# Who makes the low parts of the right operands: VectorE alone, or VectorE and GpSimd in turn

## What is computed

```
first_block:  x += mix(differential attention, forgetting attention) @ w_out
              x += (silu(h2 @ w_gate) * (h2 @ w_up)) @ w_down      # width 2816 = 22 tiles of 128
              rmsnorm
second_block: x += mix(two convolutions, stick-breaking attention) @ w_out
              x += square(relu(h2 @ w_ff1)) @ w_ff2                # width 4096 = 32 tiles of 128
              rmsnorm
```

## Time and profile before

| | us |
|---|---|
| median of 3 runs | 2449.29 (2448.19 to 2449.95) |
| the profiled execution, its own time | 2449.95 |
| its span, first to last instruction | 2447.9 |
| PE busy in the span | 2386.8 (98%) |
| DVE busy | 1906.9 (78%) |
| POOL busy | 1178.2 (48%) |
| mean granted TensorE clock | 0.989 |

### The profile page before, as it was taken

The page is one execution under the profiler, slowest core; times in us unless marked ns, Lnnn a source line. Parts: engine busy times, 40 slices in busy tenths (PEclk is TensorE's granted clock), DMA queues, the critical chain, the costliest instruction groups (busy, mean ns, idle before and its releaser), DMA issues.

```text
span 2447.9 us, 31946 instructions
## 1 busy us (share of the span) xinstructions
PE 2386.8 (98%) x11378; PEld 1953.2 (80%) x11378; DVE 1906.9 (78%) x2456; ACT 1098.3 (45%) x1885; POOL 1178.2 (48%) x798
## 2 busy tenths in 40 slices
PE   9999999999989999999999999999998999999998
PEld 7777788878768888878877878887876888788886
DVE  6777757673699787779979966778289888899976
ACT  6454656562543333344336436555163333544423
POOL 4666542211555555555545463431256555555552
PEclk9999999999999999999999999999998999999998
DMA  4311321232113232355332872223213444654522
GB/s 164 78 54 51 88 61 40 60 116 71 56 48 129 86 112 96 120 177 159 113 94 81 189 171 61 60 60 109 76 57 130 169 144 149 215 181 138 181 78 103
DMA packets 233260, 264.64 MB, mean 108 GB/s; under 512 B 18448, under 2 KB 145168, under 8 KB 232976
## 3 DMA queue, kind: packets, MB, share of 16 engines
q1 hardware_dynamic: 229504, 250.29, 32.5%
q0 software_dynamic: 3168, 11.54, 2.5%
q10 hardware_dynamic: 432, 0.79, 0.1%
HBM read 170.53 MB, written 61.60 MB: 95 GB/s over the span
## 4 chain that ended last, share of the span: by engine, by line
PE 84%; DVE 8%; POOL 3%; ACT 2%; issue 2%; DMA 1%; SPq 0%; POOLq 0%; DVEq 0%; ACTq 0%
PE PS L1768 24%; PE PS L1773 23%; PE PS L1770 23%; PE PS L1866 3%; PE PS L1853 2%; PE PS L1887 2%; PE PS L1884 2%; PE PS L1847 2%; DVE R0f L2173 1%; PE PS L1850 1%; DVE R L2180 1%; POOL stage L2650 0%; DVE R L2249 0%; PE PS L1852 0%; DVE X L2257 0%
## 5 line engine op out<-in xcount | busy, mean ns | idle before, releaser
L1768 PE MATMUL PS<-R,wh 128*128 128x512 f32 x2860 | 1137.4, 398 | 23.3 <-DVE stage L2161 10.8
L2626 POOL TENSOR_TENSOR lows<-values,wh 128x512 fp32r<-128x512 f32 (+2 forms) x483 | 717.5, 1490 | 890.0 <-ACT wh L2378 679.1
L1773 PE MATMUL PS<-R,wh 128*128 128x512 f32 x2860 | 1122.0, 392 | 8.7 <-DVE R L2180 5.9
L1770 PE MATMUL PS<-R,lows 128*128 128x512 f32 x2496 | 977.4, 392 | 1.2 <-POOL lows L2626 1.2
L1768 PEld LDWEIGHTS PS<-R,wh 128*128 128x128 f32 x2860 | 541.2, 189 | 137.8 <-DVE stage L2161 12.7
L1773 PEld LDWEIGHTS PS<-R,wh 128*128 128x128 f32 x2860 | 540.0, 189 | 129.4 <-DVE R L2180 7.1
L2378 ACT ACTIVATE wh<-values 128x512 fp32r<-128x512 f32 (+2 forms) x484 | 299.3, 618 | 580.6 <-PE PS L1773 552.3
L1770 PEld LDWEIGHTS PS<-R,lows 128*128 128x128 f32 x2496 | 471.4, 189 | 93.4 <-issue 3.8
L2257 DVE TENSOR_TENSOR X<-PS,X 128x1024 f32<-128x1024 f32 x168 | 204.2, 1217 | 35.8 <-PE PS L1773 35.3
L2626 POOL TENSOR_TENSOR late_r<-late,wh 128x512 fp32r<-128x512 f32 (+1 forms) x92 | 137.2, 1492 | 113.8 <-DVE values L2155 65.6
L2161 DVE TENSOR_TENSOR stage<-PS,stage 128x512 f32<-128x512 f32 x156 | 105.5, 685 | 64.5 <-PE PS L1773 64.3
(11 more groups left out here) (277 smaller groups left out, 3091.0 us busy)
## 6 DMA issues: line engine op xcount, KB each, us to landing
scr_hid<-R1f SPq DMA_DIRECT2D x177, 256.0 KB, 3.0
R0f<-scr_hid SPq DMA_DIRECT2D x92, 256.0 KB, 3.6
values<-w_in_dram SPq DMA_DIRECT2D x88, 256.0 KB, 2.8
R1f<-scr_hid SPq DMA_DIRECT2D x85, 256.0 KB, 3.3
values<-w_ff_dram SPq DMA_DIRECT2D x62, 256.0 KB, 3.0
values<-w_ff_dram SPq DMA_DIRECT2D x100, 128.0 KB, 2.4
R<-R SPq DMA_DIRECT2D x96, 128.0 KB, 2.3
X<-X POOLq DMA_DIRECT2D x22, 512.0 KB, 5.6
```

The costliest lines, as they stand in the source:

```text
L1768: e.matmul(PS[:, b, :], wh, high, start=s["start"], stop=False, skip_group_check=on)
L1770: e.matmul(PS[:, b, :], wl, high, start=False, stop=False, skip_group_check=on)
L1773: m = e.matmul(PS[:, b, :], wh, low, start=False, stop=s["stop"], skip_group_check=on)
L2626: e.tensor_tensor(T.wl[piece.v][:, 0:m], T.wv[piece.v][:, 0:m], T.wh[:, piece.h, 0:m].bitcast(F), ALU.subtract).then_inc(*sg.up("w_lo", pi ...
```

## The change

Of each pair of operands, the low part of one is now made by POOL and of the other by DVE. Which of the two it is alternates with the product's slot in `FROM_HIDDEN`; for a single operand (the short chunk) even slots go to POOL and odd ones to DVE. In the plain part the second of each pair goes to POOL. The planner then makes new lists for all engines. Nothing else changes: the same operands, loads, high parts and matmuls.

```diff
         def fetch_block(c, name):
             k, rows = todo[c]
             slot = FROM_HIDDEN.index(name)
-            by = ("vector", "vector")
+            by = ("vector", "gpsimd") if slot % 2 else ("gpsimd", "vector")
             fetch((c, slot), [(n, k // 2 + x, slot) for x, n in enumerate(operands(c)[name])], by)
 
         def fetch_plain(x):
             p = (tiles - 4) // 2
-            fetch(("plain", x), [(PLAIN[tag][2 * x + h], p + x // 2, 2 * (x % 2) + h) for h in range(2)], ("vector", "vector"))
+            fetch(("plain", x), [(PLAIN[tag][2 * x + h], p + x // 2, 2 * (x % 2) + h) for h in range(2)], ("vector", "gpsimd"))
```

## The result

The changed kernel takes 2466.51 us (median of 4 runs, 2465.25 to 2467.24), the kernel before 2449.62 beside it: ratio 1.007, 95% interval 1.0058 to 1.0084. It is slower by 0.7%, outside my range, and on the side to which I gave 0.17. The profiled execution took 2464.84 us.

What follows compares the result with a forecast made beforehand. PE was taken as the bound, so only its waits at the seams could give: 2.3 us before the first block products plus 1.25 in the short chunk, 3.55 us less, forecast 2445.7 us against the median; overall range 2439.5 to 2455.

Steps and rivals of the forecast that it cites:

- What POOL takes on: Full chunks: seven more parts, 8.9 to 12.5 us, bring POOL to 28 to 33 of 38.1 us; costed at nothing.
- POOL is late with the weights: Rival, chance 0.13: first weight part late in 22 groups, 0.8 us each, 17 us in all; about 2463 us.
- Both engines get in each other's way: Rival, chance 0.04: full chunks, DVE's parts and sums slowed by POOL; up to 6.3 us a chunk, halfway 2461 us.
- The seam: Before each FFN's first block product: DVE frees the bank sooner, PE waits 1.15 us less, twice 2.3 us.
- The next part takes the gap: Rival, chance 0.17: another ready part precedes the seam's sum, only the short chunk gives 1.25 us; about 2448 us.
- The short chunk: Freeing some 2 us of DVE there removes PE's waits of 0.41 and 0.84 us: 1.25 us less.
- What DVE is rid of: Full chunks: DVE loses seven parts, 6.7 us at the mean, falling from about 37 to 30 us; costed at nothing.
- The clock: At each seam, a shorter wait may keep the clock from falling: 0 to 1.7 us, in the range only.

Runs made afterwards that it cites:

- e3: The changed kernel, planner counting 1779 ns instead of 1379 for POOL's operand part and DVE's as ending after the POOL instruction beside it: 2452.87 us.
- h2: The changed kernel's lists kept, but POOL fills its 89 low parts with zeros in eight pieces of 64 columns instead of the difference: 2445.36 us.
- e2: Lists of the kernel before kept, planned with all parts on DVE; only afterwards the 89 parts are carried into POOL's list: 2448.39 us.
- f2: The changed kernel with the last seven's sum put ahead of the operand parts before it in DVE's list, at both seams: 2466.51 us.
- f4: The kernel before, with the last seven's sum put ahead of the two operand parts before it in each FFN: 2447.82 us.
- e1: The changed kernel with ACT in POOL's place for the 89 parts, writing a plain copy instead of the difference, lists planned anew: 2446.25 us.
- g3: The kernel before, all parts on DVE, planner counting DVE's operand part as ending 0.1 us behind the POOL instruction beside it: 2442.95 us.
- g1: The changed kernel's lists kept, but POOL fills each of its 89 low parts with zeros in one memset instead of the difference: 2444.1 us.
- e4: The changed kernel with the parts of each FFN's first chunk back on DVE, the other 75 on POOL: 2459.13 us.
- g4: The changed kernel with its planner counting 0.4 us more for POOL's operand part and DVE's part as it did: 2466.51 us.

## Why the prediction was wrong

**The step that failed** is "What POOL takes on", in which I wrote "I cost the move at nothing". It priced the part between 1277 and 1786 ns and took the low end for the room ("the idle 5.50 us hold four of them"). Measured: 1.74 us in the median and 1.62 in the mean. Four of those are 6.5 to 7 us, not 5.2. And it said that one operand part in front of a weight part "just fits; two do not", without asking how many the new list would put there: three or four, in 10 of 24 groups, laid out at 1.38 us each. e3, which lays out as many at the time that they take, gives back 13.6 of the 17 us: the cost of a part was the term that failed, and with it the trust in a list made from the lower one.

**POOL is late with the weights**, the rival with 0.13, is what happened, 2463 against 2466.51. Place and sign are right: waits of 1770 at groups' starts. The price of 0.8 us at 22 groups is not: in the full chunks of both FFNs PE falls back by 8.8 us at 1770, by 4.7 at 1768, where it waits for block adds, and by 1.0 at 1773. "The planner counts 1379 ns for what can take 1.79" named the cause; I took it for a few tenths.

**Both engines get in each other's way**, 0.04, is the other half. I priced it by DVE alone (a mean of 1.40 us for its 15 pieces). DVE stayed within the chunk, 36.15 of 38.10 us. POOL, whose pieces grow from 1.30 to 1.74 us in the median, ran full. I had weighed the lock on the engine that lost work instead of on the one that got it. The Trainium skill (page "SBUF — State Buffer", section "SBUF: two separate sides") states that the exclusion holds between a DVE instruction with two SBUF inputs and a GpSimd one that reads SBUF. The traces agree on both sides of it: block adds keep 1.21 us, and of DVE's 88 operand parts in h2 the 19 that run beside POOL's fills alone, which read nothing, take 676 to 693 ns, while the 63 that run beside one of its differences take up to 1823. Its page "Perfetto Trace Analysis" (section "Optimizing Scalar/DVE Operations") warns that moving work between the two might not help; 0.25 us less on DVE for 1.67 more on POOL is this case's number for it.

**The seam.** I expected 1.15 us less at each, and 3.66 and 3.18 us came in place of 1.95 and 1.89: three parts in front of the sum. "The next part takes the gap" was the rival here, in a stronger form than I gave it. e2 shows that the arithmetic held for lists that stay (0.83 us, and the clock at 1.00 over 1089 to 1095). f2 and f4 show that the gain would have been lost again in the chunks anyhow.

**The short chunk.** Forecast -1.25, measured -2.9 us: both waits are gone, and the clock's fall as well.

**What DVE is rid of** at nothing inside the chunks: right, by e1.

What stays open: how much of the loss POOL's longer hold and the mutual delay each cause in the new lists, which no run separates beyond the estimate under h2; and whether a planner that knows when both engines read SBUF at once, for every difference and not only for operand parts, would make the move pay. e3 is still 4.6 us over the runs of the kernel before beside it (2448.24), and I have no list made for the move that beats g3.

## What to carry to other kernels

Before work is moved to an idle engine, ask what the two engines share while both run: here a part that takes 0.68 us on DVE alone and 1.3 on POOL alone takes up to 1.8 on either beside the other (1.2 in the mean on DVE, 1.6 on POOL), so the idle engine's room must be counted at the overlapped price. Where a planner writes the order, a change of owner is a change of all lists, and a price that is too low by 0.2 to 0.4 us shows up not at the moved step but in front of whatever stands behind it; hold the lists and move the work (e2), and hold the lists and take the contention away (h2), to tell the two apart. Here a wrong price had to be mended for both engines at once. And measure what a stand-in costs before relying on it: eight fills of 0.15 us kept POOL busy for 0.74.

## What the runs showed of the hardware

- A POOL difference of 128x512 from SBUF takes 1.27 us at least, a POOL fill of 512 columns 0.53 us and one of 64 columns 0.15 us, but eight of these in a row 0.74 to 0.77 us. The fills did not slow down beside DVE (516 to 541 ns over all 89 of g1):

```profile
L2639 POOL MEMSET R<- x89: 516/527/541, 1076.1 to 2343.9; 128x512 f32 x89
```

- DVE's difference is held up only beside one of POOL's. In the kernel before, 70 of its 177 operand parts have no difference on POOL beside them and take 674 to 685 ns; the other 107 take 674 to 1830, 1.17 us in the mean.

- How long PE waits does not decide by itself whether the clock falls. Behind a wait of 1.95 us at the first seam it fell to half in e1 (0.83 over 10 us, as before the change); behind one of 1.94 us at the same place in e4 it stayed at full speed, and so it did in g4 behind 2.3 us. The stretches, e1 first. My "The clock" step took a shorter wait for what would keep it; the runs don't say what does.

```profile
1089.00:1099.00 10.00, 8.07 (x29) 6.54 (x30) 7.92 (x9) 6.62 (x13) 3.54 (x3) 0.83 0.77 245
```

```profile
1089.00:1099.00 10.00, 10.00 (x45) 8.24 (x46) 9.69 (x10) 6.73 (x13) 6.63 (x5) 1.00 0.92 299
```
